# Order of attention scores, outputs and small products beside the dense steps of a hybrid layer

## The chip, the cores and the metric

The kernel runs on one core of one Trainium2 chip. The core has a matrix engine (TensorE, in the profile PE, with its weight loads as PEld), a vector engine (VectorE, DVE), a scalar engine (ScalarE, ACT), a general engine (GpSimd, POOL) and a queue that issues transfers (SyncE, SP). Each engine works through its own list of instructions in order; between engines there are only semaphores. The metric is the device time of one execution in microseconds, lower is better. Time before: 908.31 us, the median of 3 runs (907.72 to 908.86).

## What is computed

The reference is a block of two hybrid layers followed by a block of two attention and feed-forward layers, on 256 tokens of width 1024, all in float32. The change is in the hybrid layers:

```python
def hybrid_layer(x, ...):
    proj = x @ w_in
    (rq, rk, rv, rg, nq, nkc, nvc, nks, nvs, nkw, nvw, ng, ngl, lx, lg) = jnp.split(proj, IN_SPLIT_POINTS, axis=-1)
    y_ret = retention(rq, rk, rv) * jax.nn.silu(rg)
    y_nsa = nsa(nq, nkc, nvc, nks, nvs, nkw, nvw, ngl, ...) * jax.nn.silu(ng)
    y_lru = rg_lru(lx, ...) * jax.nn.silu(lg)
    y = jnp.concatenate([y_ret, y_nsa, y_lru], axis=-1) @ w_out
    return layer_norm(DEEPNORM_ALPHA * x + y, ln_g, ln_b)
```

`nsa` is sparse attention with 8 heads and three branches: on compressed keys and values (15 blocks of 32 tokens, made by a product with `cmp_w`), on selected blocks (with 4 blocks and a choice of 16 all of them are selected) and on a window. Each branch is `softmax(q k) v`, and the three are summed with gates. `retention` has 4 heads: products of queries and keys times a decay, then with the values, then a normalisation. `rg_lru` is a gated linear recurrence.

## The kernel before

**Dense products.** All weights (142.8 MB) stream through a ring. SP loads a chunk into `w_raw`, ACT rounds it into `w_hi` (L1384), DVE subtracts to get `w_lo` (L1866), and PE makes three products for each piece: in token form with 512 columns (L746 to L748, about 0.23 us apart) and in feature form with 256 (L777 to L779, about 0.12 apart). `chunk_steps` hands these out in small steps: a step is three token products or six feature products, 0.7 us either way.

**The hybrid layer.** `hybrid(l)` on PE first runs the blocks with the attention's operands. Then it weaves the attention into the dense steps of the other blocks: `ahead(n)` issues the next n steps, between them stand the small products. The order is written out by hand. There are 16 units, one for each head and each of two branches (selected and window); a pair of units, one for each of two heads, shares scores and outputs. For unit u PE issues `AHEAD_A[u]` steps, the transposes of the unit's softmax weights (`nsa_weight_transposes`, L956), what the table `small` has for u, `AHEAD_B[u]` steps (3 in units 2 to 9, 2 in units 10 to 13), behind odd units the outputs of the pair (`nsa_output`, L972 and L974) and the scores two pairs on (`nsa_pair_scores`, L942 and L944), then what the table `late` has.

The three kinds of product use the array in different shapes: dense products and transposes 128x128, outputs 128x64, scores 64x128.

**What hangs on what, for a unit.** Scores (PE) -> `logits`, DVE, masked minimum (L2126, L2128) -> `softmax`, ACT, exponentials (L1534, L1535) -> `gated_pair`, DVE, scaling (L2145, L2150) -> transposes (PE, L956) -> `transposed`, ACT, copy of the transposed weights into SBUF (L1541) -> outputs (PE).

**The compressed branch.** Its softmax is finished by DVE (L2405, in `hook5`). PE transposes its weights (`compressed_transposes`, L1274, in `small` of unit 6) into the bank ps7, ACT copies them to `cmp_PT` (L1713) and counts `cmp_pt`. `compressed_output(l, 0)` and `(l, 1)` (L1282) add their products to the bank of the outputs; they are in `late` of units 7 and 10. `lru_gates` (L1293, `small` of unit 7) writes ps7 too and so waits for `cmp_pt`.

**Retention.** `retention_scores` (L915), a decay by DVE (L2318), the values centred by DVE (L2337), `retention_output` (L924 to L926, `small` of unit 11), ACT's squares of it (L1743, in `hook11`), DVE's normalisation, `retained_acts` on PE (L892, `late` of unit 14) and DVE's low part of it (L2492), the first operand of the output projection.

**Order on ACT and DVE.** Both have a function `units` that goes through the 16 units; on ACT it calls for each unit `transposed(u)`, then `front[u]`, then at even units `softmax(u + 2)` and `softmax(u + 3)`, then `hooks[u]`:

```python
transposed(u)
...
if u in front:
    front[u]()
...
if u + 3 < n and u % 2 == 0 and u and not (ph == 3 and u == 6):
    softmax(u + 2)
    softmax(u + 3)
if u in hooks:
    hooks[u]()
```

The weight splits (L1384, L1866) of blocks further on are called in the hooks.

Of the kernel before, what the change touches and what calls it, by code (L numbers as in the profile page):

```python
# [103 lines left out]
def build(nc, dram, out):  # L104
# [124 lines left out]
    with ctx:  # L229
# [465 lines left out]
        def _(pe):  # L695
# [575 lines left out]
            def compressed_transposes(l):  # L1271
                pe.wait_ge(cmp_weighted, l + 1)
                for t in range(TT):
                    mm = pe.transpose(ps7[:, 128 * t:128 * t + 128], cmp_L[:, 128 * t:128 * t + 128], ident[:, :])  # L1274
                mm.then_inc(cmp_t, 1)
# [20 lines left out]
            def hybrid(l):  # L1296

                gemms(f"in{l}", 2)
                f, o = FIRST[f"in{l}"], FIRST[f"out{l}"]
                part(f + 2, 0)  # L1300
                if l == 0:
                    pe.wait_ge(ident_in, 16)
                nsa_transposes(l, (0, 1), 2)
                part(f + 2, 1)
                nsa_transposes(l, (2, 3, 4), 2)

                def dense():
                    for b in range(f + 3, f + 7):
                        for j in range(2):
                            yield from chunk_steps(b, j)  # L1310
                    yield from token_steps(o, 0, (0, 1, 6, 7))
                    yield from token_steps(o + 1, 0, (0, 1))

                rest = dense()

                def ahead(count):
                    for _ in range(count):
                        next(rest)

                ahead(4)  # L1320
                nsa_transposes(l, (5,), 3)
                nsa_pair_scores(l, 0)
                ahead(3)
                nsa_pair_scores(l, 1)
                ahead(3)
                small = {6: lambda: compressed_transposes(l), 7: lambda: lru_gates(l), 9: lambda: retention_scores(l, (0, 1)), 10: lambda: retention_scores(l, (2, 3)),
                         11: lambda: retention_output(l)}
                late = {0: lambda: compress(l), 1: lambda: compressed_operands(l), 2: lambda: compressed_scores(l),
                        7: lambda: compressed_output(l, 0), 8: lambda: retention_transposes(l),
                        10: lambda: compressed_output(l, 1), 14: lambda: retained_acts(l)}  # L1330
                for u in range(16):
                    ahead(AHEAD_A[u])
                    nsa_weight_transposes(l, u)
                    if u in small:
                        small[u]()
                    ahead(AHEAD_B[u])
                    if u % 2:
                        nsa_output(l, u // 2)
                        if u // 2 + 2 < 8:
                            nsa_pair_scores(l, u // 2 + 2)  # L1340
                    if u in late:
                        late[u]()
                for _ in rest:
                    pass
                tokens(o, 0, (2, 3))
                tokens(o + 1, 0, (2, 3, 6, 7))
                for i in range(2):
                    tokens(o + i, 0, (4, 5))
                pair(o, lambda: normalized_acts(l, 0), (1, 1), 1, [1])
# [23 lines left out]
        def _(act):  # L1373
# [308 lines left out]
            def hybrid(l):  # L1682
                gemms(f"in{l}", 2)
                b = FIRST[f"in{l}"] + 2
                splits(b, 0)
                act.wait_ge(vec_out, 32)
                nsa_transposed(l, 0)
                take(b, 0)
                take(b, 1)
                nsa_transposed(l, 2)  # L1690
                nsa_transposed(l, 4)
                splits(b, 1)
                units(l, 16, start="both")
                units(l, 16, start="second pair")

                def retention_gate():
                    for half in range(2):
                        act.wait_ge(acc_free[half], free_count(b + 4))
                    act.activation(y[:, :, 0:256], proj[:, :, COL["rg"]:COL["rg"] + 256], ACT.Tanh, scale=0.5).then_inc(tanh_done, 1)

                def hook1():
                    take(b + 1, 0)
                    take(b + 1, 1)

                def hook5():
                    take(b + 2, 0)
                    take(b + 2, 1)
                    act.wait_ge(cmp_l, l + 1)
                    act.activation(cmp_L, cmp_L, ACT.Exp).then_inc(cmp_p, 1)

                def front6():
                    act.wait_ge(cmp_t, l + 1)
                    act.activation(cmp_PT, ps7[:, 0:256], ACT.Copy).then_inc(cmp_pt, 1)  # L1713

                def hook6():
                    splits(b + 2, 1)

                def front2():
                    if l == 0:
                        lru_exponentials()  # L1720

                def hook7():
                    lru_gates(l)

                def front8():
                    act.wait_ge(o_ready, 2 * l + 1)
                    act.activation(held, ps6[:, :], ACT.Copy).then_inc(held_done, 1)

                def hook8():
                    take(b + 3, 0)  # L1730
                    act.wait_ge(stg_ps, STG0[l] + 7)
                    act.activation(ret_T[:, 0:2, :].rearrange("p c n -> p (c n)"), ps7[:, :], ACT.Copy).then_inc(stg_a, 1)
                    splits(b + 3, 0)

                def hook9():
                    lru_decay(l)
                    take(b + 3, 1)

                def hook11():
                    lru_root(l)  # L1740
                    retention_gate()
                    act.wait_ge(ro_ps, l + 1)
                    act.activation(ret_squares, ps7[:, :], ACT.Square).then_inc(ro_squares, 1)  # L1743

                def hook13():
                    splits(b + 4, 0)
                    take(b + 4, 0)

                def hook14():
                    mixed_hi(l, 0)  # L1750
                    lru_operand(l)

                units(l, 16, {0: lambda: splits(b + 1, 0), 1: hook1, 2: lambda: splits(b + 1, 1), 3: lambda: splits(b + 2, 0), 5: hook5,
                              6: hook6, 7: hook7, 8: hook8, 9: hook9, 10: lambda: splits(b + 3, 1), 11: hook11,
                              13: hook13, 14: hook14}, front={2: front2, 6: front6, 8: front8})
                take(b + 4, 1)
                mixed_hi(l, 1)
                splits(b + 4, 1)
                mixed_hi(l, 2)
# [896 lines left out]
```

## Time and profile before

| | |
|---|---|
| median of 3 runs | 908.31 us (907.72 to 908.86) |
| profiled execution | 907.32 us |
| its span in the profile | 905.5 us |
| PE busy | 895.9 us (99%), 5666 products |
| PEld, weight loads | 768.5 us (85%) |
| DVE busy | 625.0 us (69%) |
| ACT busy | 488.7 us (54%) |
| POOL busy | 40.2 us (4%) |
| transfers | 155.55 MB, mean 172 GB/s |
| layer 0, units 0 to 15 | about 52 to 122 us |
| layer 1, units 0 to 15 | about 190 to 260 us |

How to read it: times of the profile are counted from the start of the span. In a timeline a row has the start, the duration, engine, line and operation, what is written and read, the number of instructions merged, and in brackets how long the engine was idle before it and for whom it waited. Products overlap in the records, so the time that a product costs is read from start to start, and a wait shows as a start that comes later than usual, often by more than the idle time in brackets.

### The profile page before, as it was taken

How to read it: one execution, taken by the hardware profiler on the slowest of the kernel's cores; microseconds unless marked ns; L12 is line 12 of the kernel's file. 1: busy time of each engine (PE TensorE's matmuls, PEld its weight loads, DVE VectorE, ACT ScalarE, POOL GpSimd, SP SyncE). 2: the span in 40 equal slices, each digit the busy share in tenths (PEclk: the TensorE clock that was granted, in tenths of full speed). 3: DMA queues.
4: the chain of work that ended last, by engine and by line, in shares of the span. 5: the costliest groups of instructions: out<-in, count | busy, mean ns of one | idle time of the engine just before them, and what ended most of it. 6: DMA issues, size and time to landing. Idle time of an engine off the chain costs nothing.

```text
span 905.5 us, 13952 instructions
## 1 busy us (share of the span) xinstructions
PE 895.9 (99%) x5666; PEld 768.5 (85%) x5666; DVE 625.0 (69%) x1081; ACT 488.7 (54%) x730; POOL 40.2 (4%) x69
## 2 busy tenths in 40 slices
PE   8999999999999999999999999999999999999998
PEld 7987888997888888877999988888877799998886
DVE  5679978779978998786766644456788586664441
ACT  6555746655746755565655543346567465554330
POOL 3500010000000000100000000000000000000000
PEclk9999999999999999999999999999999999999999
DMA  8953454632354568642565555657463375555540
GB/s 300 321 187 93 138 186 128 215 132 93 112 169 143 182 213 252 187 140 55 178 188 186 187 188 185 213 162 233 135 209 120 93 229 187 186 187 188 185 161 24
DMA packets 79407, 155.55 MB, mean 172 GB/s; under 512 B 5608, under 2 KB 7816, under 8 KB 79344
## 3 DMA queue, kind: packets, MB, share of 16 engines
q1 hardware_dynamic: 75152, 142.81, 48.4%
q0 software_dynamic: 4192, 11.85, 4.8%
q8 instruction: 45, 0.74, 0.3%
q14 instruction: 18, 0.15, 0.0%
HBM read 153.54 MB, written 1.11 MB: 171 GB/s over the span
## 4 chain that ended last, share of the span: by engine, by line
PE 85%; DVE 8%; ACT 4%; issue 1%; DMA 1%; SPq 1%; DVEq 0%; ACTq 0%
PE ps L746 17%; PE ps L748 16%; PE ps L747 16%; PE ps L777 8%; PE ps L779 8%; PE ps L778 8%; DVE w_lo L1866 3%; ACT w_hi L1384 1%; DMA w_raw<-in_w_in 1%; PE ps_mid L956 1%; PE ps_mid L972 1%; PE ps L1047 1%; PE ps_mid L942 1%; ACT y_tok L1507 1%; PE ps_mid L1241 1%
## 5 line engine op out<-in xcount | busy, mean ns | idle before, releaser
L1866 DVE TENSOR_TENSOR w_lo<-w_raw,w_hi 128x2048 fp32r<-128x2048 f32 (+1 forms) x134 | 302.3, 2261 | 159.7 <-ACT w_hi L1384 159.6
L1384 ACT ACTIVATE w_hi<-w_raw 128x2048 fp32r<-128x2048 f32 (+1 forms) x134 | 252.9, 1890 | 196.3 <-PE ps L748 141.9
L746 PE MATMUL ps<-w_hi,act_hi 128*128 128x512 f32 (+1 forms) x446 | 177.8, 399 | 1.9 <-DVE w_lo L1866 1.6
L748 PE MATMUL ps<-w_hi,act_lo 128*128 128x512 f32 (+1 forms) x446 | 171.0, 383 | 0.0
L747 PE MATMUL ps<-w_lo,act_hi 128*128 128x512 f32 (+1 forms) x446 | 170.8, 383 | 0.0
L746 PE MATMUL ps<-w_hi,hid 128*128 128x512 f32 x296 | 116.2, 393 | 0.1
L748 PE MATMUL ps<-w_hi,hid 128*128 128x512 f32 x296 | 115.3, 390 | 0.0
L747 PE MATMUL ps<-w_lo,hid 128*128 128x512 f32 x296 | 115.2, 389 | 0.0
L777 PE MATMUL ps<-act_hi,w_hi 128*128 128x256 f32 x384 | 110.8, 289 | 0.4 <-DVE act_lo L2065 0.4
L778 PE MATMUL ps<-act_lo,w_hi 128*128 128x256 f32 x384 | 107.6, 280 | 0.0
L779 PE MATMUL ps<-act_hi,w_lo 128*128 128x256 f32 x384 | 107.5, 280 | 0.0
L746 PEld LDWEIGHTS ps<-w_hi,act_hi 128*128 128x128 f32 x446 | 83.8, 188 | 20.4 <-issue 3.4
L748 PEld LDWEIGHTS ps<-w_hi,act_lo 128*128 128x128 f32 x446 | 83.7, 188 | 16.8
L747 PEld LDWEIGHTS ps<-w_lo,act_hi 128*128 128x128 f32 x446 | 84.0, 188 | 13.8
L777 PEld LDWEIGHTS ps<-act_hi,w_hi 128*128 128x128 f32 x384 | 72.3, 188 | 3.4 <-issue 2.0
L778 PEld LDWEIGHTS ps<-act_lo,w_hi 128*128 128x128 f32 x384 | 72.5, 189 | 0.0
L779 PEld LDWEIGHTS ps<-act_hi,w_lo 128*128 128x128 f32 x384 | 72.4, 189 | 0.0
L777 PE MATMUL ps<-early_acts,w_hi 128*128 128x256 f32 x256 | 71.8, 280 | 0.6 <-issue 0.3
L779 PE MATMUL ps<-early_acts,w_lo 128*128 128x256 f32 x256 | 71.5, 279 | 0.0
L778 PE MATMUL ps<-early_acts,w_hi 128*128 128x256 f32 x256 | 71.5, 279 | 0.0
L746 PEld LDWEIGHTS ps<-w_hi,hid 128*128 128x128 f32 x296 | 55.6, 188 | 12.6 <-DVE w_lo L1866 0.7
L748 PEld LDWEIGHTS ps<-w_hi,hid 128*128 128x128 f32 x296 | 55.5, 188 | 11.7
(369 smaller groups left out, 1239.6 us busy)
## 6 DMA issues: line engine op xcount, KB each, us to landing
w_raw<-in_ffn_w SPq DMA_DIRECT2D x64, 1024.0 KB, 5.4
w_raw<-in_w_in SPq DMA_DIRECT2D x22, 1024.0 KB, 5.5
w_raw<-in_a_w_qkv SPq DMA_DIRECT2D x18, 1024.0 KB, 5.2
w_raw<-in_b_w_qkv SPq DMA_DIRECT2D x12, 1024.0 KB, 5.0
w_raw<-in_w_out SPq DMA_DIRECT2D x8, 1024.0 KB, 4.9
w_raw<-in_b_w_o SPq DMA_DIRECT2D x4, 1024.0 KB, 4.9
w_raw<-in_w_in SPq DMA_DIRECT2D x8, 256.0 KB, 5.2
w_raw<-in_w_in SPq DMA_DIRECT2D x4, 512.0 KB, 3.4
```

What stands on the lines that cost most here:

```text
L746: pe.matmul(o, ah, wh, start=first, stop=False)
L747: pe.matmul(o, ah, wl, start=False, stop=False)
L748: mm = pe.matmul(o, al, wh, start=False, stop=last)
L777: pe.matmul(o, wh, ah, start=k == 0 and f % 2 == 0, stop=False)
L778: pe.matmul(o, wh, al, start=False, stop=False)
L779: mm = pe.matmul(o, wl, ah, start=False, stop=k == 7 and f % 2 == 1)
L942: pe.matmul(ps23[:, 512 * e:512 * e + S], q[e][:, 128:256], k[e][:, :], start=True, stop=True)
L956: mm = pe.transpose(ps4[:, 128 * i:128 * i + 128], nsa_weights(u)[:, at:at + 128], ident[:, :])
L972: pe.matmul(o[64 * e:64 * e + 64, :], v(0), nsa_PT[:, e, 0:S], start=p % 4 == 0, stop=False)
L1047: mm = pe.transpose(t_bank(2, u, g)[:, 128 * i:128 * i + 128], dil_weights(u)[:, at:at + 128], ident[:, :])
L1384: act.activation(w_hi[:, c % RING, :, 0:n], w_raw[:, c % RAW, :, 0:n], ACT.Copy).then_inc(w_hi_done, 1)
L1866: dve.tensor_tensor(lo, w_raw[:, c % RAW, :, 0:n], hi.bitcast(F), ALU.subtract).then_inc(w_lo_done, 1)
```

## The change

Four things in the PE's order, in both hybrid layers: the scores stand in front of the outputs in units 1 to 11; the compressed transposes of unit 6 and the retention outputs of unit 11 stand behind the unit's second group of dense steps, in front of scores and outputs, not ahead of it; the second compressed outputs are in unit 11, not in unit 10. One thing on ACT: the copy into `cmp_PT` is the first part of `hook6` in place of `front6`.

```diff
@@ -1323,21 +1323,23 @@
-                small = {6: lambda: compressed_transposes(l), 7: lambda: lru_gates(l), 9: lambda: retention_scores(l, (0, 1)), 10: lambda: retention_scores(l, (2, 3)),
-                         11: lambda: retention_output(l)}
+                small = {7: lambda: lru_gates(l), 9: lambda: retention_scores(l, (0, 1)), 10: lambda: retention_scores(l, (2, 3))}
+                between = {6: lambda: compressed_transposes(l), 11: lambda: retention_output(l)}
                 late = {0: lambda: compress(l), 1: lambda: compressed_operands(l), 2: lambda: compressed_scores(l),
                         7: lambda: compressed_output(l, 0), 8: lambda: retention_transposes(l),
-                        10: lambda: compressed_output(l, 1), 14: lambda: retained_acts(l)}
+                        11: lambda: compressed_output(l, 1), 14: lambda: retained_acts(l)}
                 for u in range(16):
                     ahead(AHEAD_A[u])
                     nsa_weight_transposes(l, u)
                     if u in small:
                         small[u]()
                     ahead(AHEAD_B[u])
+                    if u in between:
+                        between[u]()
                     if u % 2:
-                        nsa_output(l, u // 2)
                         if u // 2 + 2 < 8:
                             nsa_pair_scores(l, u // 2 + 2)
+                        nsa_output(l, u // 2)
                     if u in late:
                         late[u]()
@@ -1708,11 +1710,9 @@
-                def front6():
+                def hook6():
                     act.wait_ge(cmp_t, l + 1)
                     act.activation(cmp_PT, ps7[:, 0:256], ACT.Copy).then_inc(cmp_pt, 1)
-
-                def hook6():
                     splits(b + 2, 1)
@@ -1752,7 +1752,7 @@
-                              13: hook13, 14: hook14}, front={2: front2, 6: front6, 8: front8})
+                              13: hook13, 14: hook14}, front={2: front2, 8: front8})
```

## Rows read from the trace of the kernel before

**Rows 1.** The page: busy time of PE, and its granted clock in 40 slices.
```profile
PE 895.9 (99%) x5666; PEld 768.5 (85%) x5666; DVE 625.0 (69%) x1081; ACT 488.7 (54%) x730; POOL 40.2 (4%) x69
...
PEclk9999999999999999999999999999999999999999
```

**Rows 2.** The waits of PE: engine, line, for whom, us in total, times, longest.
```profile
PE ps L746 <- DVE w_lo L1866: 1.6, 1, 1.6
```

**Rows 3.** Timeline of PE, layer 0, units 5 to 7.
```profile
76.16 0.39 PE L748 MATMUL ps<-w_hi,act_lo 128*128 128x512 f32 x1
76.94 0.65 PE L972 MATMUL ps_mid<-area 128*64 128x256 f32 x4 [0.39 <-ACT area L1541]
...
79.41 0.49 PE L956 MATMUL ps_mid<-ident,y_tok 128*128 128x128 f32 x3
80.21 0.44 PE L1274 MATMUL ps<-ident,area 128*128 128x128 f32 x2 [0.31 <-DVE area L2405]
...
83.57 1.03 PE L1293 MATMUL ps<-area,tables 128*128 128x256 f32 x4
```

**Rows 4.** Timeline of ACT, layer 0, units 5 and 6.
```profile
76.33 0.47 ACT L1541 ACTIVATE area<-ps_mid 128x384 f32<-128x384 f32 x1
...
80.69 0.38 ACT L1713 ACTIVATE area<-ps 128x256 f32<-128x256 f32 x1 [0.26 <-PE ps L1274]
82.63 0.51 ACT L1534 ACTIVATE area<-area,ttr_min 128x256 f32<-128x256 f32 x1 [1.56 <-DVE ttr_min L2128]
...
84.41 1.90 ACT L1384 ACTIVATE w_hi<-w_raw 128x2048 fp32r<-128x2048 f32 x1
```

**Rows 5.** Timeline of DVE, layer 0, units 3 to 6.
```profile
67.17 2.29 DVE L1866 TENSOR_TENSOR w_lo<-w_raw,w_hi 128x2048 fp32r<-128x2048 f32 x1 [0.67 <-ACT w_hi L1384]
...
79.73 0.43 DVE L2405 TENSOR_TENSOR area<-area,cmp_weights 128x256 f32<-128x256 f32 x1
...
81.96 0.42 DVE L2126 CUSTOM_DVE_ANT_0 area<-ps_mid,tables 128x256 f32<-128x256 f32 x1
```

**Rows 6.** Timeline of PE, layer 1, unit 7.
```profile
220.87 1.03 PE L1293 MATMUL ps<-area,tables 128*128 128x256 f32 x4
```

**Rows 7.** Timeline of ACT, layer 1, unit 6.
```profile
219.85 0.51 ACT L1534 ACTIVATE area<-area,ttr_min 128x256 f32<-128x256 f32 x1 [1.34 <-DVE ttr_min L2128]
...
221.62 1.90 ACT L1384 ACTIVATE w_hi<-w_raw 128x2048 fp32r<-128x2048 f32 x1
```

**Rows 8.** Timeline of PE, layer 0, units 10 and 11.
```profile
103.49 0.28 PE L778 MATMUL ps<-act_lo,w_hi 128*128 128x256 f32 x1
103.61 0.28 PE L779 MATMUL ps<-act_hi,w_lo 128*128 128x256 f32 x1
103.82 1.08 PE L1282 MATMUL ps_mid<-area 128*64 128x256 f32 x8
104.83 0.39 PE L777 MATMUL ps<-act_hi,w_hi 128*128 128x256 f32 x1
105.06 0.28 PE L778 MATMUL ps<-act_lo,w_hi 128*128 128x256 f32 x1
...
110.66 0.39 PE L974 MATMUL ps_mid<-area 128*64 128x128 f32 x4
110.97 0.70 PE L942 MATMUL ps_mid<-area 64*128 64x256 f32 x4
```

**Rows 9.** Timeline of DVE, layer 0, units 10 to 15.
```profile
104.64 0.69 DVE L2337 TENSOR_TENSOR area<-area,st 128x512 f32<-128x512 f32 x1
...
111.94 0.42 DVE L2126 CUSTOM_DVE_ANT_0 y_tok<-ps_mid,tables 128x256 f32<-128x256 f32 x1 [0.26 <-PE ps_mid L944]
...
122.03 0.68 DVE L2492 TENSOR_TENSOR hid<-ps,hid 128x512 fp32r<-128x512 f32 x1
```

**Rows 10.** Timeline of ACT, layer 0, unit 11.
```profile
110.46 0.58 ACT L1743 ACTIVATE area<-ps 128x512 f32<-128x512 f32 x1
```

**Rows 11.** Timeline of PE, layer 0, first product of the output projection.
```profile
122.86 0.47 PE L746 MATMUL ps<-w_hi,hid 128*128 128x512 f32 x1
```

## The prediction

> **What bounds the kernel now.** I read the page first, then the waits of the matrix engine (PE), then the timelines of PE, ScalarE (ACT) and VectorE (DVE) through units 5 to 15 of both hybrid layers. PE is busy 895.9 of 905.5 us, at a granted clock of nine tenths or more in all forty slices [rows 1]. Its list of waits holds 13 small ones: the longest, 1.6 us early in the kernel [rows 2], is not touched; two are at the changed places, 0.4 us in front of a pair of outputs (L972) and 0.3 us in front of the compressed transposes (L1274) [rows 3]. So the kernel is bound by PE's own queue: what PE waits longer, the end gets later, and only what shortens this queue helps. Shares of busy time say nothing on such an edit; its price is read from which engine is last at each wait that moves.
>
> **The two waits that the change can take away** are both in layer 0 [rows 3]. In unit 5 the last dense product starts at 76.16 and the outputs at 76.94; a place without a wait has 0.32 between these (in layer 1 and in unit 7), so 0.46 us is lost. They wait for ACT's copy of the transposed weights, which ends at 76.33 + 0.47 = 76.80 [rows 4]; PE starts 0.14 after that. With the scores in front this copy has long been done, and the scores themselves wait for nothing: the logits that free their bank are those of units 6 and 7, whose softmaxes ACT has finished before that copy. In unit 6 the weight transposes start at 79.41 and the compressed ones at 80.21, where 0.33 is the time without a wait: 0.47 us lost, on DVE. Behind two, here three, dense steps this wait is gone. Layer 1 has neither. Taken alone this is 0.93 us.
>
> **The wait that the change makes.** The compressed transposes of unit 6 feed an ACT copy into cmp_PT. Before, that copy stood in `front6`, ahead of the softmaxes of units 8 and 9; now it stands in `hook6`, behind them, since `units` calls the softmaxes between front and hooks. Those softmaxes wait for DVE. And PE's `lru_gates`, right behind the transposes of unit 7, waits for cmp_pt, because its products overwrite the bank that the copy reads. In layer 0 the first softmax starts at 82.63, after 1.56 idle on DVE, and ACT is free again at 84.41, where today the next weight split (L1384) starts [rows 4]. DVE's logits of unit 8 start at 81.96 [rows 5] in an unbroken row of DVE work that goes back to the split at 67.17, which waited for ACT, and hangs on nothing that PE does sooner, so this time stays. The copy takes 0.38 [rows 4]: cmp_PT is ready at 84.79, and with the 0.14 that PE took after the other ACT copy the gates start at 84.93. Today they start at 83.57 [rows 3]. PE would be there at about 82.6 (83.57 less the 0.93 above) and idles for 2.3 us; the 0.93 saved is inside this idle time and worth nothing. Net 84.93 - 83.57 = **+1.36**.
>
> In layer 1 the same: PE comes to the gates at 220.87 [rows 6], ACT is done with the softmaxes at 221.62 [rows 7], copy 222.00, gates 222.14. Net **+1.27**.
>
> Bounds of the latency from ACT to PE: 0.05 (the compressed transposes started that long after DVE's product ended, 79.73 + 0.43 [rows 5]) and 0.24 (0.1 more than the outputs took, an estimate, since the gates' first weight load is 128 columns wide and theirs 64). So each of the two terms moves by 0.1 either way. Queued behind the wait are all of PE's later work in the layer; DVE next asks for its results at the copy of the retention keys, which comes later by the same amount. DVE's logits of units 10 and 11 need PE's scores of unit 7: they are finished at about 89.7 then, DVE wants them at 90.5, no further loss. The split behind the copy on ACT comes 0.3 later and DVE needs its result 1.7 later still.
>
> **The second compressed outputs** go from behind unit 10 to behind the outputs of unit 11. Where they stand now they cost 0.21 from the last dense product, 1.01 for themselves and 0.23 to the second dense product, where plain dense products have 0.12 each: 1.45 for what would be 0.24, so 1.21 in all [rows 8]. Behind outputs with the same shape of array (128x64) their 8 products cost 8 x 0.12 = 0.96 and one change of shape is gone, since those outputs now have 0.31 from L974 to the scores for four 128-wide products of 0.06 [rows 8]. I work it out to 0.94 against 1.21: **-0.27** a layer. Bounds: 0 (if the joint is as dear as the two changes were) and -0.35. In unit 7 the first compressed outputs then also follow outputs, not scores: **-0.08** (bound 0 to -0.1).
>
> **Scores in front of outputs** is in itself neutral: the same products with the same three changes of shape, dense to one, to the other, back to dense. Bounds -0.1 and +0.1 for the six pairs of a layer together. No DMA, no queue of SP or POOL and no instruction is added.
>
> **Retention outputs** go behind two dense steps. They issue the same products on both sides of the move, with one change of shape behind them where the scores had it: 0 (bounds -0.1 and +0.1). They wait for DVE's centred values, ready at 104.64 + 0.69 = 105.33 [rows 9]. Their new place, from the dense product at 103.61: one step, transposes, two steps, 0.12 + 0.71 + 0.33 + 1.5, is 106.2 in the same clock, 0.9 behind. Their 24 products of 0.11 (three transposes take 0.33) end near 109; ACT comes to its square of them behind two table loads and a tanh at 110.46 [rows 10]: not late either. The retained transposes of unit 14 keep 0.26 of their 0.3 us of slack.
>
> **What is late next, at the end of the layer.** DVE waits 0.26 for the scores of unit 11 [rows 9]; these now come 2 us sooner, so DVE runs 0.26 ahead from there. The first product of the output projection waits for DVE's retention low part, 122.03 + 0.68 = 122.71, and starts 0.15 after it [rows 9, 11]. There DVE is last, so of the 0.27 of the compressed outputs only DVE's 0.26 counts.
>
> **The sum.** Layer 0: 1.36 - 0.08 - 0.26 = +1.02. Layer 1: 1.27 - 0.08 - 0.26 = +0.93. Together **+1.95 us**. Behind each layer PE is the bound again and the start of the next stage hangs on PE, so nothing gives it back. The profiled execution took 907.32 (span 905.5 and 1.8 around it); it would take 909.3. It stands 0.99 below the median of the runs, 908.31, which becomes **910.3 us**. The bounds of the terms give +1.6 to +2.9; with 0.6 either side for the spread of runs the forecast's own range is 909.3 to 911.8.
>
> **Rivals.**
> 1. *The copy isn't late: the saved waits count.* If the softmaxes of units 8 and 9 began early enough for the copy behind them to end by 82.6 (layer 0) and 220.8, the sum would be -0.93 - 2 x 0.34 = -1.6, 906.7 us: not slower. For it speaks that DVE is 69% busy over the whole span; against it that it has no gap between 67.17 and 84, and that in layer 1 the softmax's start (219.85) is set by the end of the dense block that PE itself does. It decides from a shift of 2.2 us of DVE's work. Chance 0.08.
> 2. *The idle time lowers PE's clock.* The granted clock is full in all slices, also in the one with the idle 1.6 us ahead of the product at 19.76 [rows 1, 2]; here 2.3 us are idle. If the clock fell to the lower level (1.2 for 2.4 GHz) for some 6 us after one of the two gaps, half of that is lost: +3 more, 913.3 us. The nearest row is against it. [...] Chance 0.05.
> 3. *DVE or ACT becomes the bound behind the stall*, at unit 14, where the retained transposes have 0.3 us of slack, or at the scores of unit 7 with 0.8: 0.5 to 1 us more a layer, 911.8 us. Chance 0.10.
> 4. *Forecast*: 0.77.
>
> **Chances.** What a measurement of this kernel can tell from no change is about 0.2%, 1.8 us, and the forecast lies just beyond: of its 0.77 I give 0.43 to slower and 0.34 to the same, the latter with short latencies. Rivals 2 and 3 add 0.15 to slower; rival 1 is 0.05 same and 0.03 faster. Slower 0.58, same 0.39, faster 0.03. Range for 8 in 10: 908.9 to 912.0.
>
> **What would show it.** In the profile after: a wait of PE at L1293 in both layers, 2.0 to 2.5 us and 1.1 to 1.4, put down to ACT's copy into cmp_PT; this copy directly behind the softmax of unit 9; no wait left at L972 of unit 5 and at L1274; no gap of DVE ahead of the logits of unit 14; L1282 directly behind L974 twice a layer. The prediction is wrong if L1293 starts without a wait, if PE's clock is below nine tenths in any slice, or if a wait appears behind unit 7 that before had none.

## The result and the profile after

The changed kernel takes **910.77 us** (median of 12 executions, 909.49 to 911.91). The kernel before, run beside it, takes 908.31 us (median of 11; a twelfth execution of it took 3131.5 us and is left out). The ratio is 1.0026, with a 95% interval of 1.0019 to 1.0034: slower by 2.5 us. The forecast was 910.3, and the whole interval lies above no change.

The page and PE's waits of the kernel after. ACT's and DVE's line numbers are two higher than before up to the copy into `cmp_PT`, which is now L1715; the weight split is L1386.

```profile
PE 897.1 (99%) x5666; PEld 769.6 (85%) x5666; DVE 625.5 (69%) x1081; ACT 489.1 (54%) x730; POOL 40.3 (4%) x69
...
PEclk9999999999999999999999999999999999999999
...
PE ps L1293 <- ACT area L1715: 3.3, 2, 2.2
PE ps L746 <- DVE w_lo L1866: 1.2, 1, 1.2
```

A new wait heads the list: the gate products (L1293) wait twice for the moved copy, 3.3 us together. The waits at L972 and L1274 [rows 3] are gone. The page's line on the clock looks as before [rows 1], though its slices are 23 us long, and below that matters.

The timeline of PE, layer 0, units 5 to 7:

```profile
76.21 0.39 PE L748 MATMUL ps<-w_hi,act_lo 128*128 128x512 f32 x1
76.53 0.70 PE L942 MATMUL ps_mid<-area 64*128 64x256 f32 x4
...
77.38 0.65 PE L972 MATMUL ps_mid<-area 128*64 128x256 f32 x4
...
81.41 0.39 PE L1274 MATMUL ps<-ident,area 128*128 128x128 f32 x2
...
82.32 0.49 PE L956 MATMUL ps_mid<-ident,y_tok 128*128 128x128 f32 x3
84.98 1.20 PE L1293 MATMUL ps<-area,tables 128*128 128x256 f32 x4 [2.17 <-ACT area L1715]
85.97 1.91 PE L1293 MATMUL ps_mid<-area,tables 128*128 128x256 f32 x4
87.33 0.99 PE L746 MATMUL ps<-w_hi,act_hi 128*128 128x512 f32 x1
88.11 0.63 PE L747 MATMUL ps<-w_lo,act_hi 128*128 128x512 f32 x1
88.54 0.63 PE L748 MATMUL ps<-w_hi,act_lo 128*128 128x512 f32 x1
...
89.34 0.39 PE L747 MATMUL ps<-w_lo,act_hi 128*128 128x512 f32 x1
```

The timeline of ACT in the same stretch:

```profile
82.71 0.51 ACT L1536 ACTIVATE area<-area,ttr_min 128x256 f32<-128x256 f32 x1 [2.69 <-DVE ttr_min L2128]
...
84.48 0.36 ACT L1715 ACTIVATE area<-ps 128x256 f32<-128x256 f32 x1
84.74 1.90 ACT L1386 ACTIVATE w_hi<-w_raw 128x2048 fp32r<-128x2048 f32 x1
```

The transposes that feed the copy (L1274) are issued at 81.41, and ACT is idle until 82.71. It could copy then, but next in its list are the softmaxes that wait for DVE. They start at 82.71 (before 82.63 [rows 4]), the copy at 84.48, the gates at 84.98. In layer 1 it is the same with half the idle time. Timelines of PE and of ACT, layer 1:

```profile
224.80 1.10 PE L1293 MATMUL ps<-area,tables 128*128 128x256 f32 x4 [1.10 <-ACT area L1715]
```

```profile
222.52 0.51 ACT L1536 ACTIVATE area<-area,ttr_min 128x256 f32<-128x256 f32 x1 [1.61 <-DVE ttr_min L2128]
...
224.29 0.36 ACT L1715 ACTIVATE area<-ps 128x256 f32<-128x256 f32 x1
```

The last rows of PE's timeline above show a second thing. Behind the stall, dense products last 0.63 us and start 0.43 apart, not 0.39 and 0.23, until 89.3. The windows of the same kernel (busy time by engine, granted clock in the column between POOL and the last two):

```profile
85.00:86.00 1.00, 1.00 (x5) 0.84 (x6) 0.96 (x3) 1.00 (x1) 0.00 (x0) 0.93 0.00 0
86.00:87.00 1.00, 1.00 (x4) 0.82 (x3) 1.00 (x2) 1.00 (x2) 0.00 (x0) 0.50 0.00 0
87.00:88.00 1.00, 1.00 (x4) 0.82 (x3) 0.96 (x5) 0.09 (x2) 0.00 (x0) 0.50 0.00 0
88.00:89.00 1.00, 1.00 (x4) 0.71 (x4) 1.00 (x3) 1.00 (x3) 0.00 (x0) 0.50 0.06 16
89.00:90.00 1.00, 1.00 (x5) 0.86 (x4) 1.00 (x1) 1.00 (x3) 0.00 (x0) 0.86 0.00 0
```

The granted clock fell to 0.50, the lower level (1.2 GHz), for some 3.4 us behind the idle stretch.

**Where the time went**, read by aligning the same products in both traces. A shift is start after less start before. The gates are compared with the unit ahead of them that had not moved yet: in layer 0 with the start (+0.09), in layer 1 with unit 7 (+2.67).

| place | shift | change of it | forecast of the term |
|---|---|---|---|
| unit 1 to 4, layer 0 | +0.09 | | |
| transposes of unit 7, layer 0 | -0.93 | -1.02 | -0.93, eaten |
| gates, layer 0 | +1.41 | +1.32 against the start | +1.36 |
| transposes of unit 8 | +3.01 | +1.60: clock and unit 7 | -0.08 |
| transposes of unit 12 | +2.61 | -0.40 | -0.27 |
| layer 1 begins | +2.72 | +0.11 | ends at DVE: -0.26 in all |
| gates, layer 1 | +3.93 | +1.26 | +1.27 |
| transposes of unit 8 | +3.84 | -0.09 | -0.08 |
| transposes of unit 12 | +3.46 | -0.38 | -0.27 |
| layer 1 ended | +3.54 | +0.08 | ends at DVE: -0.26 in all |
| end of the span | +4.35 | +0.81 | 0 |

Two of these changes had no term: the clock (1.65 us with unit 7's -0.05 taken out), and 0.8 us that arise between 440 and 520 us, far behind the change.

Because of the clock, single executions can't be compared without their mean granted clock. The executions of most kernels fall into two groups, at 1.0 and at 0.998; for the kernel before, which has the most, these lie 1.7 to 1.8 us apart. In the table the kernels that ran together stand under the row of the kernel before that ran beside them (mean of the executions at each clock, in brackets their count; at most two of a kernel showed 0.999 and stand in neither column, nor do two of e5, told of below; of the executions of the kernel before that ran beside the first result no clock is on record):

| kernel | ratio to before, 95% | at 1.0 | at 0.998 |
|---|---|---|---|
| changed | 1.0026 (1.0019-1.0034) | 909.83 (5) | 911.45 (7) |
| *before* | | 907.59 (14) | 909.25 (10) |
| e1_front6 | 0.9978 (0.9968-0.9988) | 905.33 (4) | 907.26 (4) |
| e2_hook_only | 1.0031 (1.0019-1.0043) | 910.62 (3) | 911.72 (2) |
| e3_filler | 1.0019 (1.0010-1.0028) | 909.31 (5) | 910.79 (5) |
| e4_after_again | 1.0025 (1.0015-1.0035) | 909.09 (1) | 911.14 (8) |
| *before* | | 908.16 (15) | 910.00 (12) |
| e9_front6_early | 0.9975 (0.9966-0.9985) | 906.66 (11) | none |
| e10_after_early | 1.0023 (1.0012-1.0034) | 910.08 (5) | 911.86 (6) |
| e5_copy_late | 1.0079 (1.0063-1.0095) | none | 915.64 (3) |
| e7_scores_first | 0.9992 (0.9981-1.0003) | 907.23 (6) | 909.05 (6) |
| *before* | | 907.78 (18) | 909.45 (14) |
| e6_gates_between | 0.9983 (0.9974-0.9992) | 906.31 (4) | 907.37 (6) |
| e8_cmp11 | 0.9990 (0.9980-1.0000) | 906.87 (7) | 908.83 (5) |
| e11_no_transposes | 0.9988 (0.9977-0.9999) | 906.59 (7) | 908.65 (5) |
| e12_front6_again | 0.9979 (0.9968-0.9989) | 905.70 (5) | 907.69 (6) |

### The profile page after: what moved, and what is told of

It reads as the page before. It is cut to its first block, busy times and chain, and to the rows that moved or that the text cites. A ratio compares the mean times of both kernels' runs of the same rounds, so it can differ in the third digit from the quotient of the medians.

```text
span 909.9 us, 13952 instructions
## 1 busy us (share of the span) xinstructions
PE 897.1 (99%) x5666; PEld 769.6 (85%) x5666; DVE 625.5 (69%) x1081; ACT 489.1 (54%) x730; POOL 40.3 (4%) x69
## 4 chain that ended last, share of the span: by engine, by line
PE 84%; DVE 8%; ACT 4%; issue 1%; DMA 1%; SPq 1%; DVEq 0%; ACTq 0%
PE ps L746 16%; PE ps L748 16%; PE ps L747 16%; PE ps L777 8%; PE ps L778 8%; PE ps L779 8%; DVE w_lo L1866 3%; ACT w_hi L1386 1%; DMA w_raw<-in_w_in 1%; PE ps L1047 1%; PE ps_mid L956 1%; PE ps_mid L972 1%; PE ps_mid L942 1%; ACT y_tok L1509 1%; PE ps_mid L1241 1%
## 5 line engine op out<-in xcount | busy, mean ns | idle before, releaser
L1386 ACT ACTIVATE w_hi<-w_raw 128x2048 fp32r<-128x2048 f32 (+1 forms) x134 | 253.2, 1892 | 196.3 <-PE ps L748 142.6
L746 PE MATMUL ps<-w_hi,act_hi 128*128 128x512 f32 (+1 forms) x446 | 178.7, 401 | 1.7 <-DVE w_lo L1866 1.2
L746 PE MATMUL ps<-w_hi,hid 128*128 128x512 f32 x296 | 116.2, 393 | 0.2
L746 PEld LDWEIGHTS ps<-w_hi,act_hi 128*128 128x128 f32 x446 | 84.1, 188 | 20.8 <-issue 3.6
L746 PEld LDWEIGHTS ps<-w_hi,hid 128*128 128x128 f32 x296 | 55.6, 188 | 12.6 <-DVE w_lo L1866 0.8
```

What stands on the lines that cost most here:

```text
L746: pe.matmul(o, ah, wh, start=first, stop=False)
L1386: act.activation(w_hi[:, c % RING, :, 0:n], w_raw[:, c % RAW, :, 0:n], ACT.Copy).then_inc(w_hi_done, 1)
```

## The experiments

**1. The copy put back, all else kept (e1, and e12 on another occasion).**

```diff
-                def hook6():
+                def front6():
                     act.wait_ge(cmp_t, l + 1)
                     act.activation(cmp_PT, ps7[:, 0:256], ACT.Copy).then_inc(cmp_pt, 1)
+
+                def hook6():
                     splits(b + 2, 1)
...
-                              13: hook13, 14: hook14}, front={2: front2, 8: front8})
+                              13: hook13, 14: hook14}, front={2: front2, 6: front6, 8: front8})
```

> The changed order of PE with ACT's copy into cmp_PT back in front of the softmaxes of units 8 and 9. Theory (all that the change loses comes from this copy's place): no wait at the retained gates L1293, PE's clock full in every execution, and 1.6 us below the kernel before (0.93 from the two waits of layer 0, 0.34 a layer from the compressed outputs and DVE's 0.26). Rival (scores in front of outputs or the retention outputs' new place cost something themselves): level with the kernel before or above it, with PE waits at L942, L972 or L924.

> The same kernel as the changed one with the copy in front, beside the two above on the same chip, as their measure: ratio 0.9978 to the kernel before (0.9968 to 0.9988), 2.3 us under it at equal clock. If it comes out at 0.999 or above, the gain first measured was the chip's and not the kernel's.

Measured: 0.9978 and 0.9979, 2.3 us under the kernel before at clock 1.0 the first time and 2.1 the second, more than the 1.6 that the theory of e1 gave. By the shifts of the two profiles it is 2.0 and 1.9 from unit 3 of layer 0 to the end of layer 1: 1.5 and 1.4 in layer 0 and 0.5 in layer 1, where 1.27 and 0.34 were expected. And the theory's full clock in every execution was missed: 4 of 10 executions are at 0.998 in e1 and 6 of 12 in e12, though nothing stalls at the gates. This version beats both kernels. No wait is left at the gates, as the timelines of PE and ACT of e1 show:

```profile
82.28 1.03 PE L1293 MATMUL ps<-area,tables 128*128 128x256 f32 x4
```

```profile
81.45 0.39 ACT L1715 ACTIVATE area<-ps 128x256 f32<-128x256 f32 x1 [1.81 <-PE ps L1274]
82.28 0.51 ACT L1536 ACTIVATE area<-area,ttr_min 128x256 f32<-128x256 f32 x1 [0.45 <-DVE ttr_min L2130]
```

ACT copies inside the time in which it waits for DVE anyway. So the order on PE is a gain of 0.2%, and the one line on ACT turns it into a loss.

**2. The copy moved, nothing else (e2).** The kernel before with the reverse of the edit above.

> The kernel before with ACT's copy moved behind the softmaxes and nothing else. Theory: PE waits at L1293 for 1.1 to 1.4 us in both layers, +2.6 us on the kernel before, as no saved wait is lost in it. With idle times this short the clock stays full if the fall hangs on the length of the gap (2.2 us in layer 0 of the changed kernel): all executions in one group. Rival (any gap at this place can bring the clock down): two groups, some executions 1.6 us longer, with a mean clock of 0.998.

Measured: 1.0031, +3.0 us at clock 1.0 (3 executions against 14), where 2.6 were expected; the shifts of its profile come to 2.75. In the profile the shift grows by 1.33 at layer 0's gates and by 1.26 at layer 1's, by 1.42 and 1.33 up to unit 8. PE's wait for the copy:

```profile
PE ps L1293 <- ACT area L1713: 2.3, 2, 1.2
```

Against the units before, the gates come about as late as with the whole change (there 1.32 and 1.26), though PE's order saves nothing here; its idle time is shorter by just what that order saves. This confirms the step "the 0.93 saved is inside this idle time". On the clock the run says little: 2 of 5 executions are at 0.998, not all in one group as the theory had it, but in the profile, which is one of the two, the fall comes at 20 us and not at the gates.

**3. The stall filled with products that nobody reads (e3).** Behind the transposes of unit 7, in front of the wait for `cmp_pt`:

```diff
+                for _ in range((4, 2)[l]):
+                    pe.matmul(ps5[:, 0:S], gate_w[:, l, 1, 0, :], lru_w[:, 0, 0, :], start=True, stop=True)
```

> The changed kernel with 4 (layer 0) and 2 (layer 1) products of 0.43 us each in front of PE's wait for cmp_pt, written to the gates' second bank and overwritten by the gates. They leave PE 0.4 us idle. Theory (the idle time lets the clock fall, which is what separates the two groups of executions of the changed kernel): all executions with full clock, in the lower group, 1.4 us above the kernel before, and L1293 starts at the same time as without them. Rival (the two groups have another cause): still two groups 1.6 us apart. If the fillers are on the path: 1.7 and 0.9 us more.

Measured: 1.0019, 909.31 at clock 1.0, and the wait is 0.3 us:

```profile
PE ps L1295 <- ACT area L1717: 0.3, 1, 0.3
```

Work in the gap leaves the lateness of the gates nearly as it is (1.24 and 1.16 by the shifts); that the median is 1.1 us under that of the changed kernel beside it (909.67 and 910.78) is mostly the mix of clocks, 5 of 11 executions at 0.998 against 8 of 9. The theory wanted every execution at full clock. 5 of 11 is about the share of the kernel before (10 of 24 here), and so the stall couldn't be the only source of falls.

**4. The changed kernel again (e4).**

> The changed kernel once more, beside the others on the same chip. Theory: two groups of executions, 1.6 us apart, by mean clock 1.000 and 0.998, about half in each; the lower group 1.4 us above the kernel before. Rival (the groups belong to the day or the chip): one group.

Measured: 1.0025. There are two groups again, but of 8 executions and 1, not half and half; they lie 2.05 us apart, and the one at 1.0 is 1.5 above the kernel before. The profile has the stall, 2.1 us at the gates of layer 0, but no fall of the clock behind it. It has one at 21 us instead. Windows of e4:

```profile
20.00:21.00 1.00, 0.58 (x3) 0.53 (x4) 0.27 (x1) 1.00 (x1) 0.00 (x0) 1.00 0.07 12
21.00:22.00 1.00, 1.00 (x5) 0.74 (x4) 0.69 (x1) 1.00 (x3) 0.00 (x0) 0.67 0.53 78
22.00:23.00 1.00, 1.00 (x4) 0.81 (x3) 1.00 (x1) 0.78 (x1) 0.00 (x0) 0.50 0.98 329
...
86.00:88.00 2.00, 0.81 (x4) 0.77 (x5) 1.93 (x4) 2.00 (x6) 0.00 (x0) 1.00 0.00 0
```

This is behind the early wait at L746, which the kernel before has too [rows 2]. The kernel before shows 0.998 in 36 of the 87 executions that ran beside experiments, the changed kernel in 15 of 21. The next two kernels take the sources apart.

**5. The early gap filled (e9: on e1; e10: on the changed kernel).** Behind the bias product at 18 us, in both:

```diff
                 pe.matmul(ps7[0:24, 0:384], relb[:, :], hot[0:32], start=True, stop=True).then_inc(vec_ps, 1)
+                for _ in range(6):
+                    pe.matmul(ps4, act_hi[:, 7, 0:128], act_hi[:, 6:8, :].rearrange("p k n -> p (k n)"), start=True, stop=True)
```

> The changed kernel with ScalarE's copy of the compressed weights back in front of unit 6's softmax, and six products of an earlier operand, whose results nobody reads, put behind the bias product at about 18.5 us, where the PE otherwise idles for about 1.5 us. Theory (the two levels of time are falls of the PE's granted clock behind an idle stretch, here the early one): the early stretch is filled, every execution has a mean granted clock of 1.0, none lies 1.6 us above the others, and the median comes to the level that the same kernel without the six products has at clock 1.0, 905.3 us (905.0 to 905.8). Rival (the levels have another cause, and the clock shown is only a companion): four of ten executions stay at 0.998 and 907.2 us, and the median is 905.9.

> The changed kernel as it is, with the same six unread products at about 18.5 us. Theory (the stall of 1.2 to 2.2 us at the gates itself lets the clock fall in some executions, beside the early stretch): some executions, about a third to a half, still show 0.998 and about 911.4 us, the others 1.0 and 909.7; the median lies at 909.7 to 911.4, still about 2.1 us above the kernel before at clock 1.0. Rival (only the early stretch lets the clock fall, and the stall at the gates costs its own length alone): all executions at 1.0 and 909.7 us.

Measured, e9: 11 of 12 executions at 1.0, one at 0.999, none at 0.998, where the same kernel without the six products has 10 of 22 at 0.998. The early gap is the source of these. The level was missed: 906.66, 1.5 us under the kernel before and not the 2.1 to 2.3 of e12 and e1. The six products are hardly the reason: in the timeline of e9 they take until 20.10, and the dense product behind them starts then, while without them it started at 19.43 in the profile of e1 and at 20.14 in that of e12. In e9 the low parts that it waits for are ready at 17.66 + 2.29 = 19.95 anyway, as DVE's timeline shows.

```profile
18.46 1.65 PE L864 MATMUL ps_mid<-act_hi 128*128 128x512 f32 x6
20.10 0.47 PE L746 MATMUL ps<-w_hi,act_hi 128*128 128x512 f32 x1
```

```profile
17.66 2.29 DVE L1870 TENSOR_TENSOR w_lo<-w_raw,w_hi 128x2048 fp32r<-128x2048 f32 x1 [3.65 <-ACT w_hi L1388]
```

In e10 the same six products show no cost either: it is 1.9 us above the kernel before at clock 1.0, and the changed kernel without them is 1.9 above at 0.998 (911.14 and 909.25). The profile of e9 has the gain of the hybrid layers whole, 2.0 us, as e1 and e12 have, and loses 1.5 us far behind them, between 440 and 520 us and between 700 and 880 us; the last section comes back to that. Whether the other executions of e9 lost their 0.6 to 0.8 us there, no run shows. On the whole the fill takes the variation away and gains nothing: 0.9975 against 0.9978.

Measured, e10: 6 of 12 executions at 0.998, at 911.86 against 910.08. With no early gap left these falls can only be those at the gates, and its profile has one there (windows of e10):

```profile
84.00:85.00 1.00, 0.14 (x1) 0.17 (x2) 0.96 (x3) 1.00 (x5) 0.00 (x0) 0.86 0.00 0
85.00:86.00 1.00, 1.00 (x3) 0.82 (x4) 0.96 (x3) 1.00 (x1) 0.00 (x0) 0.50 0.00 0
86.00:87.00 1.00, 1.00 (x4) 0.82 (x3) 1.00 (x3) 0.89 (x2) 0.00 (x0) 0.50 0.00 0
87.00:88.00 1.00, 1.00 (x4) 0.73 (x4) 0.96 (x4) 0.00 (x0) 0.00 (x0) 0.50 0.00 0
88.00:89.00 1.00, 1.00 (x6) 0.84 (x5) 1.00 (x3) 0.52 (x2) 0.00 (x0) 0.93 0.00 0
```

In e10 the stalls cost their length always, and the clock in every second execution.

**6. The copy one step later still (e5).**

```diff
                 def hook6():
                     act.wait_ge(cmp_t, l + 1)
+                    splits(b + 2, 1)
                     act.activation(cmp_PT, ps7[:, 0:256], ACT.Copy).then_inc(cmp_pt, 1)
-                    splits(b + 2, 1)
```

> The changed kernel with ScalarE's copy one step later still, behind the 1.9 us weight split of unit 8, so that the PE stands at the gates for about 1.9 us more in each layer (about 4.1 us in layer 0, 3.0 in layer 1). Theory (each microsecond that the copy is late is a microsecond of the kernel, and a longer stall brings the clock down more often): +3.8 us on the changed kernel by the length of the stalls, and one or two falls of the clock at 1.65 us in nearly every execution: 910.8 + 3.8 + 1.0 to 2.5 = 915.6 to 917.1. Rival (later waits of the same unit absorb part of the stall, for VectorE and ScalarE work ahead in it): at most half of it, 912.5 to 913.5.

Measured: 915.95 us, 1.0079, inside the theory's range. PE's waits and PE's timeline at the gates of both layers:

```profile
PE ps L1293 <- ACT area L1716: 6.9, 2, 4.0
```

```profile
86.95 2.04 PE L1293 MATMUL ps<-area,tables 128*128 128x256 f32 x4 [3.96 <-ACT area L1716]
...
228.37 0.89 PE L1293 MATMUL ps<-area,tables 128*128 128x256 f32 x3 [2.90 <-ACT area L1716]
```

The 3.6 us by which the two waits grew (3.3 to 6.9) are all in the time: e5 lies 3.8 us above e10 at 0.998. Nothing behind the stall gives any of it back. No execution is at 1.0; one is at 0.996 and one at 0.994. Yet in the profile the clock fell at the first wait alone, while at the one of 2.90 us in layer 1 it stayed full.

**7. The gates later (e6).** The copy where the change puts it, but the gates behind unit 7's dense steps:

```diff
-                small = {7: lambda: lru_gates(l), 9: lambda: retention_scores(l, (0, 1)), 10: lambda: retention_scores(l, (2, 3))}
-                between = {6: lambda: compressed_transposes(l), 11: lambda: retention_output(l)}
+                small = {9: lambda: retention_scores(l, (0, 1)), 10: lambda: retention_scores(l, (2, 3))}
+                between = {6: lambda: compressed_transposes(l), 7: lambda: lru_gates(l), 11: lambda: retention_output(l)}
```

> The changed kernel with ScalarE's copy as late as the change puts it, but the gate products behind unit 7's dense steps (some 5 us of PE work) and no longer in front of them. Theory (the copy's being late costs nothing in itself, only the PE's having no other work until it comes): no wait at the gates, no fall of the clock behind them, and the time of the changed kernel with the copy in front: ratio to the kernel before 0.9975 (0.996 to 0.999), at clock 1.0 about 2.3 us under the kernel before. Rival (the later gates hold up the scan of the recurrence and whatever waits for it, or the banks that the copy reads hold up the next transposes): a wait of 1 us or more elsewhere in each layer, and a time at or above the kernel before.

Measured: 0.9983; at clock 1.0 it is 1.5 us under the kernel before, where e12 beside it is 2.1 under. With the late copy uncovered the difference is 3.9 us (at 0.998, 911.14 of e4 against 907.26 of e1); covered it is 0.6, or 0.3 by the shifts of the profiles. The work that covers it is three dense steps, 2.1 us, not the 5 us of the expectation. No wait has appeared elsewhere in PE's list either, as the rival would have it. So most of the price is not the copy's being late but PE's having nothing else to do. The timelines of PE and ACT show how close it still is: the copy ends at 86.03 + 0.36 = 86.39, and the gates start 0.15 behind it, 0.48 behind the last dense product.

```profile
86.06 0.39 PE L748 MATMUL ps<-w_hi,act_lo 128*128 128x512 f32 x1
86.54 1.10 PE L1293 MATMUL ps<-area,tables 128*128 128x256 f32 x4
```

```profile
86.03 0.36 ACT L1715 ACTIVATE area<-ps 128x256 f32<-128x256 f32 x1
```

**8. The parts of PE's order, alone.** Scores in front of outputs only, on the kernel before (e7):

```diff
                     if u % 2:
-                        nsa_output(l, u // 2)
                         if u // 2 + 2 < 8:
                             nsa_pair_scores(l, u // 2 + 2)
+                        nsa_output(l, u // 2)
```

> The kernel before with one part of the change alone: the score products of the next pair in front of the output products. Forecast as on record: the 0.39 us wait of unit 5's output products (layer 0 only) goes, 0.46 us with its switch, and the gain is kept only if no wait takes its place behind; 0 to -0.5 us at equal clock. Theory after the first four kernels (the gain is kept, as the shifts of the others at unit 5 say): 907.1 us at clock 1.0 against 907.6 of the kernel before, shift -0.46 from unit 5 of layer 0 to the end. Rival (the wait in front of the compressed transposes of unit 6, 0.31 us, grows by what was saved, for it ends by another engine's clock): 907.6, shift 0 from unit 6 on.

Measured: 0.9992 (0.9981 to 1.0003), at clock 1.0 0.9 us under the kernel before, more than either theory gave. In the timeline of PE the wait in front of the compressed transposes went from 0.31 [rows 3] to 0.79:

```profile
80.31 0.49 PE L956 MATMUL ps_mid<-ident,y_tok 128*128 128x128 f32 x3
81.59 0.44 PE L1274 MATMUL ps<-ident,area 128*128 128x128 f32 x2 [0.79 <-DVE area L2405]
```

It grew by the 0.46 saved one unit earlier, for it ends by DVE's clock: here the rival was right. By the shifts, the gain is elsewhere: 0.13 us between units 7 and 8 of each layer, and 0.3 at the end of each layer, where DVE's wait for the scores of unit 11 [rows 9] is gone from its list.

The second compressed outputs in unit 11 and the retention outputs behind its second dense step, on the kernel before (e8):

```diff
-                small = {6: lambda: compressed_transposes(l), 7: lambda: lru_gates(l), 9: lambda: retention_scores(l, (0, 1)), 10: lambda: retention_scores(l, (2, 3)),
-                         11: lambda: retention_output(l)}
+                small = {6: lambda: compressed_transposes(l), 7: lambda: lru_gates(l), 9: lambda: retention_scores(l, (0, 1)), 10: lambda: retention_scores(l, (2, 3))}
+                between = {11: lambda: retention_output(l)}
...
-                        10: lambda: compressed_output(l, 1), 14: lambda: retained_acts(l)}
+                        11: lambda: compressed_output(l, 1), 14: lambda: retained_acts(l)}
```

> The kernel before with two parts of the change alone: the second compressed outputs in unit 11 in place of unit 10, and the retention outputs behind unit 11's second dense step. Forecast as on record: 0.27 us in each layer, of which 0.26 is VectorE's wait at the end of layer 0. Theory after the first kernels, in all of which unit 12 comes 0.38 us early against unit 8: -0.38 in each layer, -0.75 in all at equal clock. Rival (what the mode switches and waits of unit 11 give, the wait at the layer's end takes, as the shift of -0.3 behind the layer in the kernel with scores in front alone makes possible): at most -0.2 in each layer.

Measured: 0.9990, -0.9 us at clock 1.0; the shifts fall by 0.38 in layer 0 and 0.32 in layer 1, near the theory. But only 0.21 of it stands at unit 12, the rest at the layer's end. Here the compressed outputs follow the scores and not the outputs, so one change of shape is not saved, as PE's timeline of e8 shows:

```profile
111.95 0.39 PE L944 MATMUL ps_mid<-area 64*128 64x128 f32 x4
112.27 1.08 PE L1282 MATMUL ps_mid<-area 128*64 128x256 f32 x8
```

All parts but the move of the compressed transposes, with the copy in front (e11); against e1 one line is other:

```diff
-                between = {6: lambda: compressed_transposes(l), 11: lambda: retention_output(l)}
+                between = {11: lambda: retention_output(l)}
```

(and the transposes are in `small` of unit 6 again).

> The changed kernel with ScalarE's copy in front of the softmax and the compressed transposes of unit 6 where they were before, in front of the dense step: all parts of the change but one. The scores in front alone left the wait at unit 6's transposes 0.48 us longer, all that it had gained. Theory (the two parts pay together alone: scores in front bring the gain, the transposes' move covers what VectorE still owes): here the wait at L1274 of layer 0 is about 0.8 us, and the time 0.5 us above that of the kernel with all parts and the copy in front, 906.9 to 907.4 median or 1.8 us under the kernel before. Rival (the transposes' move is worth nothing by itself): as fast as that kernel, 2.3 us under the one before.

Measured: 0.9988, at clock 1.0 1.2 us under the kernel before and 0.9 above e12. The wait at L1274 is 0.8, as expected, and the median is in its range, but at clock 1.0 the gain is 1.2 and not 1.8: the move is worth twice what I gave: it saves not only the 0.48 by which this wait had grown, but also the 0.47 that it cost from the start.

The parts don't add up. Alone they save 0.9 (e7) and 0.9 (e8), together 1.2 (e11). By the shifts each gains 0.3 to 0.4 a layer around unit 12 and the layer's end, and both together 0.33 to 0.34. That fits the forecast's step that DVE is last at the output projection and what PE gains beyond DVE's one wait is lost there.

## Why the prediction was right

By its own steps:

- **PE's queue sets the time.** Right. Every microsecond of a stall that an experiment added or took away appeared in the time (e2, e5, e1).
- **The copy comes late by the softmaxes, which hang on DVE.** Right to a tenth: the gates were put at 84.93 and started at 84.98; net 1.36 forecast, 1.32 measured; in layer 1 1.27 and 1.26. The latency of 0.14 from ACT to PE, the least certain term, was 0.14 in layer 0 (84.48 + 0.36 to 84.98) and 0.15 in layer 1.
- **The 0.93 saved is worth nothing here.** Right: e2 lacks it and its gates are no later. That it is worth something once the wait is gone, e1 and e11 show.
- **Compressed outputs.** -0.27 was forecast and -0.40 and -0.38 measured at unit 12, past the bound of -0.35. The timeline of layer 0 shows the term:

```profile
113.26 0.39 PE L974 MATMUL ps_mid<-area 128*64 128x128 f32 x4
113.48 1.03 PE L1282 MATMUL ps_mid<-area 128*64 128x256 f32 x8
114.44 0.39 PE L777 MATMUL ps<-act_hi,w_hi 128*128 128x256 f32 x1
```

  From L974 to the dense product it is 1.18, where outputs or scores alone had 0.32, so 0.86 and not 0.94; against the 1.21 of before [rows 8] this term is -0.35. It came to nothing more in the sum: the layers gave it back to 0.27 and 0.30, which is DVE's 0.26.
- **Scores in front of outputs, neutral.** Wrong by itself, right in the sum. Alone it saves almost 0.5 a layer (e7), 0.3 of it at the layer's end, for it brings unit 11's scores sooner to DVE, which waits for them. The prediction credited this 0.26 to the compressed outputs. Either part is enough, so it was counted once, and the sum was right.
- **Retention outputs, what is late next in unit 14.** Right: no wait of PE appeared there, and DVE has no gap ahead of the logits of unit 14. The slack of 0.8 us that DVE had for the scores of unit 7 held in e4, where the clock stayed full at the gates. Where the clock fell there it did not hold, as DVE's timeline of the changed kernel shows:

```profile
91.56 0.42 DVE L2126 CUSTOM_DVE_ANT_0 y_tok<-ps_mid,tables 128x256 f32<-128x256 f32 x1 [0.90 <-PE ps_mid L944]
```

  From unit 8 to the next layer the shift falls by 0.29 in the changed kernel, by 0.36 in e4 and by 0.39 in e10, which has the same wait of DVE; so no cost of it is seen.
- **The sum**, +1.95. The terms it named come to 1.32 - 0.05 - 0.27 = 1.00 (unit 7's 0.05 from e4, where the clock didn't fall behind the gates) and 1.26 - 0.09 - 0.30 = 0.87, 1.87 in all. At equal clock and side by side the changed kernel is 1.9 us above the kernel before (911.14 and 909.25 at 0.998; the single execution at 1.0 is 1.5 above), and e10 1.9 as well, at either clock. The bounds were drawn too narrow: +1.6 to +2.9 leaves out the 0.1 either way that the scores and the retention outputs were each given in each layer; with these and all the others end to end it is about +1.1 to +3.2.
- **Rival 2, the clock.** This is the step that was mis-sized: it got a chance of 0.05 as a case of its own, while at the gates it is part of every second execution (6 of 12 in e10). It rested on the page's line of 40 slices, where a fall of 3.4 us inside a slice of 23 us still reads 9, and on one execution, in which the early gap had happened to leave the clock alone. So the prediction's sign for it, a slice below nine tenths, could not have shown it. And its price was put at 3 us, from a fall of some 6 us that no run shows; ten profiles show one of 3.4 us, and half of that is 1.7. The Trainium skill ("TensorE: Matmul & The Clock Gate", section "HAM oscillation — how this bites in real kernels") describes this kind of thing, waits between groups of matmuls that bring the engine back to its lower clock. On that the trace agrees: products at 0.63 us in place of 0.39 behind an idle stretch. The waits of its example are longer, some 3 to 5 us; here 1.3 to 2.2 us were enough in part of the executions. What rule decides it, no run here shows.
- **What is left over.** The kernel before has falls as well, in 41% of executions, the changed one in 71%: 0.3 more at 1.7 us is 0.5 us, an estimate. With 1.9 that is 2.4; the medians lie 2.6 apart in e4 (910.78 and 908.16) and 2.5 in the first result. The forecast of 910.3 missed this half microsecond, which its range of 0.6 for the spread of runs took in. That the range held this is luck: the 0.6 was given for spread and not for the clock.

## What to carry to other kernels

Before an instruction is moved behind others on its engine, ask what those wait for: this copy of 0.36 us got behind softmaxes that wait for a third engine, and the matrix engine paid 1.3 us a layer. When a wait goes, ask by whose clock the next one ends: 0.46 us saved in unit 5 was lost in unit 6, until the work at that place was moved too. And where a busy matrix engine stalls, even for a microsecond or two, ask for the clock behind the stall too: compare executions at the same granted clock, and look at windows of a microsecond, not at the slices of the page.

## What the runs showed of the hardware

- The granted clock fell to 0.50 for 3.4 us at idle stretches of PE of only 1.3 to 2.2 us (3.96 in e5), in a part of the executions of one and the same kernel: 36 of 87 for the early gap, 6 of 12 for the stalls at the gates. Ten of the fourteen profiles have one such fall, seven at the early gap and three at the gates of layer 0. It began between 0.4 us before the first product behind the stretch and 1.4 us after it. A fall costs about 1.7 us (the two groups of the kernel before lie 1.66, 1.84 and 1.67 apart). A longer stretch, 2.90 us, was also seen without a fall (e5, layer 1), and so was an early gap of 1.88 us (e5), so length alone doesn't decide.
- None of the 21 executions of the changed kernel shows a mean clock under 0.998, that is, two falls; if the early gap and the gates were independent there should be some four (an estimate: 21 x 36/87 x 6/12 = 4.3). In e5 there are lower ones, 0.996 and 0.994. What ties them together stays open.
- Open as well is the 0.8 us between 440 and 520 us. There the same products start later and later, in e7 by 0.06 us every 6.4 us, at full granted clock. It is in the profiles of the changed kernel, of e4, e5, e7 and e9 (e5 and e9 lose another 0.7 us between 700 and 880 us), and not in the other eight, though e10 and e4 differ only in six early products. So it goes with the execution rather than with a part of the change; its cause stays open.
